# Expert biases summed once per expert and copied into the accumulators by ScalarE, in a one-core mixture-of-experts layer

## The reference

```python
def moe_ffn(h, w_router, b_router, w_gu, b_gu, w_down, b_down):
    ...
    top_logit, top_e = lax.top_k(logits, TOP_K)          # 4 of 32 experts for each token
    gate_w = jax.nn.softmax(top_logit, axis=-1)
    ...
    gu = lax.ragged_dot(xs, w_gu, group_sizes) + b_gu[e_sorted]
    g, u = gu[:, :EXPERT_FF], gu[:, EXPERT_FF:]
    g = jnp.minimum(g, SWIGLU_LIMIT)
    u = jnp.clip(u, -SWIGLU_LIMIT, SWIGLU_LIMIT)
    act = (u + 1) * (g * jax.nn.sigmoid(SWIGLU_ALPHA * g))
    out = lax.ragged_dot(act, w_down, group_sizes) + b_down[e_sorted]
    out = out * gate_w.reshape(-1)[order][:, None].astype(out.dtype)
    y = jax.ops.segment_sum(out, src, num_segments=n_tok)
```

## Time and profile before

| what | us |
|---|---|
| median of 3 runs | 2632.04 (2630.66 to 2635.24) |
| the profiled execution | 2637.12 |
| its span | 2635.5 |
| TensorE matmuls busy | 2398.9 (91%) |
| VectorE busy | 1545.5 (59%) |
| ScalarE busy | 1337.9 (51%) |
| GpSimd busy | 827.8 (31%) |

### The profile page before, as it was taken

The page is one execution under the profiler, slowest core; times in us unless marked ns, Lnnn a source line. Parts: engine busy times, 40 slices in busy tenths (PEclk is TensorE's granted clock), DMA queues, the critical chain, the costliest instruction groups (busy, mean ns, idle before and its releaser), DMA issues.

```text
span 2635.5 us, 55139 instructions
## 1 busy us (share of the span) xinstructions
PE 2398.9 (91%) x19125; PEld 1348.2 (51%) x19126; DVE 1545.5 (59%) x1828; ACT 1337.9 (51%) x1395; POOL 827.8 (31%) x946
## 2 busy tenths in 40 slices
PE   6999987899989959899899998889988999999991
PEld 2555554677755535455455554445544555545550
DVE  2222237566636665962943758999679615165975
ACT  1111144356632345852843658888578624165861
POOL 1122222500003353332333433434334423233322
PEclk9999988899999969999999999999999999999996
DMA  8000043430032285973954769999889825177974
GB/s 313 29 18 18 9 147 130 127 89 0 0 128 83 99 281 194 395 265 97 362 203 157 267 240 354 397 397 393 313 322 397 316 70 182 29 268 267 356 281 179
DMA packets 180248, 538.48 MB, mean 204 GB/s; under 512 B 20672, under 2 KB 37490, under 8 KB 180142
## 3 DMA queue, kind: packets, MB, share of 16 engines
q1 hardware_dynamic: 150620, 487.79, 48.9%
q0 software_dynamic: 26656, 46.85, 8.0%
q10 hardware_dynamic: 2916, 3.14, 0.4%
HBM read 493.11 MB, written 45.20 MB: 204 GB/s over the span
## 4 chain that ended last, share of the span: by engine, by line
PE 48%; DVE 6%; issue 5%; DMA 2%; ACT 2%; POOL 1%; ACTq 0%; DVEq 0%; SPq 0%; POOLq 0%
PE psum L2060 43%; DVE arena L1831 4%; PE psum L2049 2%; PE psum L2044 2%; DMA arena<-in_w_down 1%; PE psum L2038 1%; ACT arena L1653 1%; DVE arena L1925 0%; DVE arena L1890 0%; DVE arena L1926 0%; POOL expert_lists L1508 0%; DMA expert_lists<-arena 0%; DVE arena L1939 0%; DVE arena L1880 0%; ACT arena L1701 0%
## 5 line engine op out<-in xcount | busy, mean ns | idle before, releaser
L2060 PE MATMUL psum<-arena 128*64 128x512 bf16 x12528 | 1423.1, 383 | 69.6 <-DVE arena L1880 39.2
L2060 PEld LDWEIGHTS psum<-arena 128*64 128x64 bf16 x12528 | 717.2, 111 | 725.3 <-DVE arena L1831 49.1
L1831 DVE TENSOR_TENSOR arena<-arena 128x2048 bf16<-128x2048 f32 x384 | 862.8, 2287 | 186.2 <-ACT arena L1653 181.0
L1653 ACT ACTIVATE arena<-arena 128x2048 bf16<-128x2048 f32 x384 | 723.1, 1904 | 100.0 <-DVE arena L1831 69.6
L1563 POOL DMA_INDIRECT expert_sums<-arena x90 | 187.6, 2085 | 678.3 <-issue 655.7
L553 PE MATMUL psum<-arena 128*128 128x512 f32 (+2 forms) x864 | 300.6, 506 | 1.1 <-ACT arena L409 1.1
L553 PEld LDWEIGHTS psum<-arena 128*128 128x128 f32 x864 | 151.4, 191 | 134.9 <-issue 130.2
L1880 DVE TENSOR_TENSOR arena<-psum,arena 128x512 bf16<-128x512 f32 x87 | 59.8, 687 | 234.3 <-ACT arena L1695 234.3
L1534 POOL DMA_INDIRECT arena<-expert_inputs,arena x88 | 108.4, 1231 | 203.9 <-PE psum L2038 178.2
L1691 ACT ACTIVATE arena<-psum 128x1024 bf16<-128x1024 bf16 x87 | 88.6, 1018 | 156.5 <-issue 154.8
L1706 ACT ACTIVATE arena<-psum,arena 128x512 f32<-128x512 f32 x87 | 59.3, 682 | 201.6 <-PE psum L2060 201.6
(11 more groups left out here) (268 smaller groups left out, 2172.9 us busy)
## 6 DMA issues: line engine op xcount, KB each, us to landing
arena<-in_w_gu SPq DMA_DIRECT2D x256, 1024.0 KB, 18.5
arena<-in_w_down SPq DMA_DIRECT2D x128, 1024.0 KB, 15.3
arena<-in_w_ada SPq DMA_DIRECT2D x12, 2048.0 KB, 8.6
arena<-in_x_sample SPq DMA_DIRECT2D x16, 512.0 KB, 3.5
arena<-in_w_in SPq DMA_DIRECT2D x3, 2048.0 KB, 19.4
expert_sums<-arena SPq DMA_DIRECT2D x10, 512.0 KB, 6.6
expert_inputs<-arena SPq DMA_DIRECT2D x10, 512.0 KB, 2.8
x_after_mixing<-arena SPq DMA_DIRECT2D x9, 512.0 KB, 2.7
```

The lines of the kernel that those rows point to most:

```text
L1653: nc.scalar.activation(high(e, p, c), raw[p][c], ACT.Copy).then_inc(sem(f"hi_made{c}"), 1)
L1831: nc.vector.tensor_tensor(w_lo[p][c], raw[p][c], high(e, p, c), ALU.subtract).then_inc(sem(f"lo_made{c}"), 1)
L2060: last = nc.tensor.matmul(bank(b)[group(g)], parts[part][:, cols], w[:, kk, g * H:(g + 1) * H], start=False, stop=(k == KT - 1 and part == 1))
```

## The change

Three banks, `T_GATE`, `T_UP` and `T_Y`, hold the bias sums of an expert. In a first unit TensorE sums the gate and up biases into both the working bank and the T bank; for the down bias it fills the T bank alone (in the opening unit both). In units that are not first ScalarE copies the T bank into the working bank, `lay_gate` and `lay_up`, and TensorE's products go on top of it (`start=False`). The down bank is laid by ScalarE in every unit but the opening one (`lay_y`), for the down product of the unit before. New semaphores `gate_laid`, `up_laid` and `y_laid` make TensorE wait for the copies. Where no copy is needed ScalarE only raises the count. The rows of the next expert are loaded in the first unit of an expert, for gate and up after chunk 4's products, and for down after the result.

```diff
--- before.py
+++ after.py
@@ -1397,7 +1397,7 @@
 
         opening = lambda j: isinstance(j, int)
         group = lambda g: slice(64 * g, 64 * g + 64)
-        B_GATE, B_UP, B_Y, B_ACT, B_X = range(5)
+        B_GATE, B_UP, B_Y, B_ACT, B_X, T_GATE, T_UP, T_Y = range(8)
         SWISH_TOP = 7.0 / (1.0 + math.exp(-1.702 * 7.0))
 
         def high(e, p, c):
@@ -1700,6 +1700,18 @@
                         wait(act, sem("act_turned"), j)
                     nc.scalar.activation(uact, bank(B_GATE), ACT.Sigmoid, scale=1.702).then_inc(sem("sig_made"), 1)
 
+                def lay_y(j):
+                    wait(act, sem("y_made"), j + (DELAY - 1))
+                    nc.scalar.activation(bank(B_Y), bank(T_Y), ACT.Copy).then_inc(sem("y_laid"), 1)
+
+                def lay_up(j):
+                    wait(act, sem("act_made"), j)
+                    nc.scalar.activation(bank(B_UP), bank(T_UP), ACT.Copy).then_inc(sem("up_laid"), 1)
+
+                def lay_gate(j):
+                    wait(act, sem("g_made"), j)
+                    nc.scalar.activation(bank(B_GATE), bank(T_GATE), ACT.Copy).then_inc(sem("gate_laid"), 1)
+
                 def result(j):
                     act.wait_ge(sem("used11"), j + 1)
                     wait(act, sem("taken"), j * 2 + 2 * (DELAY + 1))
@@ -1719,13 +1731,19 @@
                         for at in itertools.islice(chunks, count):
                             hi(*at)
 
+                    if not first:
+                        lay_up(j)
+                    if not opening(j):
+                        lay_y(j)
                     if last:
                         divide(2 if first else 1)
                     if not opening(j):
                         act_hi(j - 1)
                     sigmoid(j)
                     if last:
-                        wait(act, sem("used4"), n)
+                        act.sem_inc(sem("gate_laid"), 1)
+                    if first and not final(e):
+                        wait(act, sem("used4"), j + 1)
                         bias_gu(e + 1)
                     divide(2)
                     if opening(j):
@@ -1735,14 +1753,21 @@
                     else:
                         keep_x(j + 1)
                     divide(2 if first else 1)
-                    if not opening(j):
+                    if not last:
+                        lay_gate(j + 1)
+                    if opening(j):
+                        act.wait_ge(sem("y_bias_made"), 1)
+                    else:
                         result(j - 1)
-                        if first:
-                            bias_dn(e)
+                    if last:
+                        act.sem_inc(sem("up_laid"), 1)
+                    if first and not final(e):
+                        bias_dn(e + 1)
                     divide(None)
 
                 expert_units_dividing(act, body)
                 T = act.value_load(tstart[0:1, NE:NE + 1], min_val=0, max_val=MAX_UNITS)
+                lay_y(T)
                 act_hi(T - 1)
                 result(T - 1)
 
@@ -2046,7 +2071,9 @@
 
                 def bias(b, rows, first):
                     for g in range(2):
-                        nc.tensor.matmul(bank(b)[group(g)], pickrow[:, (first + g) * UNIT:(first + g + 1) * UNIT], rows, start=True, stop=False)
+                        ins = nc.tensor.matmul(bank(b)[group(g)], pickrow[:, (first + g) * UNIT:(first + g + 1) * UNIT], rows,
+                                               start=True, stop=True)
+                    return ins
 
                 def product(b, parts, p, c, e1):
 
@@ -2058,16 +2085,17 @@
                         for part, w in ((0, wh), (0, wl), (1, wh)):
                             for g in range(2):
                                 last = nc.tensor.matmul(bank(b)[group(g)], parts[part][:, cols], w[:, kk, g * H:(g + 1) * H],
-                                                        start=False, stop=(k == KT - 1 and part == 1))
+                                                        start=False, stop=(k == KT - 1 and part == 1), skip_group_check=True)
                     last.then_inc(sem(f"used{c}"), 1)
 
                 x_parts = (xT[:, 0:H], xT[:, H:2 * H])
                 a_parts = (aT_hi, aT_lo)
 
-                def down(j, p, e1):
-                    wait(pe, sem("b_dn_in"), e1 * 16)
-                    wait(pe, sem("y_made"), j + DELAY)
-                    bias(B_Y, rows_dn, 0)
+                def down(j, p, e1, entering=None):
+                    wait(pe, sem("y_laid"), j + 1)
+                    if entering is not None:
+                        wait(pe, sem("b_dn_in"), entering * 16 + 16)
+                        bias(T_Y, rows_dn, 0)
                     wait(pe, sem("alo_made"), j + 1)
                     for c in range(8, 12):
                         product(B_Y, a_parts, p, c, e1)
@@ -2077,24 +2105,33 @@
                 pe.wait_ge(sem("tiles_known"), 2)
 
                 def body(e, p, j, first):
-                    wait(pe, sem("b_gu_in"), e * 16 + 16)
                     if not opening(j):
+                        pe.wait_ge(sem("gate_laid"), j)
                         wait(pe, sem("g_made"), j)
-                    bias(B_GATE, rows_gu, 0)
+                    if first:
+                        wait(pe, sem("b_gu_in"), e * 16 + 16)
+                        bias(B_GATE, rows_gu, 0)
+                        bias(T_GATE, rows_gu, 0)
                     wait(pe, sem("xT_made"), j + 1)
                     for c in range(4):
                         product(B_GATE, x_parts, p, c, e + 1)
                     if not opening(j):
                         turn_act(j - 1)
                         turn_x(j + 1)
+                        pe.wait_ge(sem("up_laid"), j)
                         wait(pe, sem("act_made"), j)
-                    bias(B_UP, rows_gu, 2)
+                    if first:
+                        bias(B_UP, rows_gu, 2)
+                        bias(T_UP, rows_gu, 2)
                     for c in range(4, 8):
                         product(B_UP, x_parts, p, c, e + 1)
                     if opening(j):
                         turn_x(j + 1)
-                    if not opening(j):
-                        down(j - 1, 1 - p if first else p, e if first else e + 1)
+                        pe.wait_ge(sem("b_dn_in"), 16)
+                        bias(B_Y, rows_dn, 0)
+                        bias(T_Y, rows_dn, 0).then_inc(sem("y_bias_made"), 1)
+                    else:
+                        down(j - 1, 1 - p if first else p, e if first else e + 1, e if first else None)
 
                 expert_units(pe, body)
                 T = pe.value_load(tstart[0:1, NE:NE + 1], min_val=0, max_val=MAX_UNITS)
```

## The result

The change made the kernel slower by 138 us: 2771.24 us (median of 4 runs, 2762.67 to 2774.77) against 2632.91 for the kernel before in the same job, a ratio of 1.0526 (95% interval 1.0511 to 1.054). The forecast was 2660, in a range up to 2683. The sign was right, the size was not. The profiled execution took 2762.67 us.

The account below looks back on a forecast made before the run. Most units were taken as bound by TensorE, single-unit experts by chunk splitting or loads. -35.6 + 6.9 + 27.8 + 23 + 6 = +28.1 us on 2637.12 gave 2665, laid on the median 2660; range 2638 to 2683.

Parts of the forecast that it names:

- The sign: Whole kernel: slower by more than what a measurement can tell from no change (5.3 us), chance 0.85.
- bias pairs gone, less the pairs added: TensorE, all units: -35.6 us for pairs removed in 55 non-first units, +6.9 for pairs added in first units.
- 15 ordinary first units, TensorE's stand: At the end of ordinary middle first units TensorE waits 1.85 us each for the gate copy, +27.8 us.
- clock after these stands: TensorE after the ordinary 1.85 us stands: counted as harmless, no lower clock, 0 us.
- 7 first units behind single-unit experts: ScalarE later there: gate waits 28.8 us, down copy 3.5, less 9.3 given back, +23; clock drops +6.
- What goes: Three bias pairs in each of 55 non-first units, 0.216 us a pair: 35.6 us saved, nearly all on the path.
- What comes on TensorE: First units sum gate and up biases twice, two pairs more, 0.43 us; 16 units on the path, +6.9 us.
- The new wait: Gate copy behind two chunks in first units that are not last: TensorE stands 0.95 + 0.34 + 0.56 = 1.85 us.
- 22 waits: Next unit's first gate product waits for the gate copy: 15 of some 1.9 us, 7 of some 4, 57 in all.
- the rival of the clock: Every one of 22 TensorE stalls sends the clock down, 1.7 us each: 37 us instead of 6, 2691; chance 0.12.
- TensorE waits for the up or the down copy in units that are not first: Named as a sign of a wrong forecast; these copies were expected to stand where ScalarE waits for TensorE's transposes.
- Table loads: ScalarE's table loads were to stay two per expert, 63 or so.

Follow-up runs that it names:

- a_shift: The changed kernel with 80 never executed instructions ahead of ScalarE's loop over experts, so its code lies elsewhere: 2694.27 us, ratio 1.0238 to the kernel before.
- c_early_shift: The changed kernel with the gate copy ahead of the two chunks in first units and 80 never executed instructions ahead of ScalarE's loop: 2627.83 us, ratio 0.9987.
- i_fill: a_shift with ten more pairs of bias matmuls ahead of the down products in each first unit: 2682.05 us, ratio 1.0188 to the kernel before.
- h_two_copies: The changed kernel with the gate copy early, the up copy kept, the down bias summed by TensorE in every unit, no dead instructions: 2630.73 us, ratio 0.9995.
- e_ahead_shift: c_early_shift with the up and down copies also moved ahead of the trailing chunks: 2638.80 us, ratio 1.0027 to the kernel before.

## Why the prediction was wrong

The sum said +28.1. a_shift has the change without the fetching of code, and its units, compared one by one with those of before over the stretch (+56.0), give each term:

| term | forecast | measured |
|---|---|---|
| bias pairs gone, less the pairs added: all units but those of the other rows | -28.7 | -30.5 |
| 15 ordinary first units, TensorE's stand | 15 x 1.85 = +27.8 | 15 x 2.37 = +35.6 |
| clock after these stands | 0 | 8 x 1.68 = +13.4 |
| 7 first units behind single-unit experts, with 5 last units that follow them, clock there included | 23 + 6 = +29 | +37.5 |
| fetching ScalarE's code again | no term | +71 (after less a_shift) |

The measured column adds up to 127, and the stretch grew by 127.3. The stand is 2.18 us of idle in the profile, which counts from the modelled end of the product before. The units grew by 2.37, and the same units without the stand, in c_early_shift, by nothing, so 2.37 is its price.

The failed step is the one that isn't there. The prediction ("What goes", "What comes on TensorE", "The new wait") counts what each engine executes, and gives the longer code of ScalarE no price, neither in the sum nor among the rivals. It is the largest term, 71 to 76 us, and alone larger than the range had room for. It is not the only failed step: without it (a_shift, 2694) the time would still have been 11 us above the upper end, by the clock and the other terms below. The rows of before could not show it (26 packets, no idle), but the loop's growth from 275 to 321 instructions stood in the change.

**Pairs.** Right. 322 matmuls, and a unit in the middle of an expert is 0.65 us shorter (3 x 0.216; 31 units, 17.34 - 16.69). Of the 30.5 us 4.3 come from the 8 single-unit experts, which together got shorter although they have pairs more and none less; why is open.

**The gate wait in ordinary first units.** The mechanism and the place were right, 22 waits, as forecast. The size was 2.37, not 1.85, just within the bounds of 1.3 to 2.4. In the rows of expert 1 the second chunk ends at 1046.91, 0.83 us ahead of the first product, where 0.56 was allowed for the copy, and so 1.54 after TensorE could have begun, where 0.95 + 0.34 = 1.29 was allowed. The copy itself took 0.58, as forecast. c_early_shift shows that this wait was the whole cost of the copy there.

**The clock.** "The ordinary 1.85 us I count as harmless" was wrong: one stand of 2.53 us that had no such end was made a rule, where the earlier trace rows already showed that one and the same wait can go either way. Of 15 stands of 2.18 us 8 were followed by the lower clock, and i_fill shows the cause. The page "TensorE: Matmul & The Clock Gate" of the Trainium skill, section "HAM oscillation", which stood beside the rival of the clock, describes waits of 3 to 5 us between bursts of matmuls; here shorter stands, of 2.18 us, did it too, in about half the places. In the ordinary first units the rival that had every stall cost 1.7 us was as far off as the forecast that had none of them do so.

**Behind single-unit experts.** 37.5 in place of 29. The prediction had the down copy at 7 x 0.5 = 3.5; a_shift's pairs wait 19.2 us for it. It takes the place of the 3.30 us that the products waited for VectorE before, so it is mostly not new; but the rest of the unit starts from there and the gate wait behind it reaches 6.19 us. And "TensorE waits for the up or the down copy in units that are not first" was named as what would make the forecast wrong: this did not happen in the changed kernel, where the gate wait is longer and hides it. It came in c_early_shift, once that was gone.

**Table loads.** 63, as forecast.

The best version is c_early_shift, 4 us under before, with an interval that just leaves out no change. The change can be made harmless. By the count of matmuls it takes 100 x 0.216 = 22 us from TensorE (10 in h_two_copies), and of this 4 us are left in c_early_shift, 2 in h_two_copies and none in e_ahead_shift, 7 us slower than before: the rest returns behind single-unit experts.

## What to carry to other kernels

Before longer code goes to an engine that loops, ask where its loop lies among the code blocks and not only how long it is: an engine idle with "issue" at the start of each turn, and more packets in the queue of instructions than before, say that it is fetched again, and dead instructions ahead of the loop are a cheap test. A copy that TensorE waits for belongs ahead of work that nobody waits for, and a stand of TensorE of 2 us was here worth its length and, in 8 of 15 places, 1.7 us at the lower clock besides.

## What the runs showed of the hardware

- A loop of 319 ScalarE instructions costs nothing at positions 573 to 892 and 63 us at 598 to 917; one of 321 costs 71 to 76 us at 591 to 912 and nothing at 676 to 997; 313 cost 67 us at 592 to 905 and nothing at 677 to 990. Each of 14 jumps back then costs 5 packets of instructions and 3.9 to 8.9 us of ScalarE.
- ScalarE copies 128x512 f32 from PSUM to PSUM in 0.56 to 0.59 us.
- 48 products behind a stand of 2.18 us took 5.37 us in 7 of 15 places and 6.98 to 7.06 in 8. Which of the two comes I could not tell from the profile; that is open.
